# Two transformers' norms at the boundaries: x turned by a product with a diagonal of inverse norms

## The chip, the cores and the metric

One core of a Trainium2 chip runs one program. The metric is the device time of one execution in microseconds (us). [...] VectorE, ScalarE and GpSimd work on vectors, and SyncE's queue issues the loads.

## The reference

Two blocks of two layers each run one after the other on x (256 tokens of 1024 features, fp32). Each of the four layers is a mixer (stick-breaking attention, forgetting attention, differential attention with a context, short convolution) and a gated feed-forward part of 2816 features. In the first block the output of each part is normed before it is added:

```python
x = x + gt * rmsnorm(o, g_post)          # first block; the second: h = h + g * y
h = modulate(rmsnorm(x, g_pre), sh, sc)  # x / sqrt(mean(x*x) + eps) * g, then * (1 + sc) + sh
```

So between every two parts there is a boundary: the product's result o is gated and added to x, x is normed over its 1024 features, scaled and shifted by columns that come from c, and goes into the next product.

## The kernel before

x lies in SBUF as two tiles of 128 tokens (t = 0, 1) by 1024 features. The products take features on partitions, so at each boundary x must be turned. There are eight boundaries with work, b = 1 to 8; b = 8 only adds. Odd ones lead from a mixer to a feed-forward part, even ones to the next mixer. Weights stream as 1 MB chunks through four buffers (`raw`); ScalarE rounds each half chunk (`whi`, line 1213), VectorE takes the rest (`wlo`, line 1720), and TensorE makes three products for each pair of such parts. Six halves are kept.

Each engine's order is written out by hand, and engines wait for counters. At a boundary, for each tile t and half c of the features:

- ScalarE squares the product o (b <= 4 alone) and, once x is updated, x, with a sum over the half (line 1268, `scalar_square`). Behind the first half it makes sum / 1024 + eps (line 1271); behind the second the logarithm (1278) and exponential (1280), which leaves the inverse norm.
- VectorE multiplies o with the gate row (`vector_gated`, 1819 and 1816), adds it to x (`vector_added`, 1828 or 1831), and scales x by the inverse norm into `xn` (`vector_scale`, 1838, two halves).
- TensorE turns `xn` in 128x128 tiles into PSUM (`transposes`, 752), by pairs p = 0 to 3 of two tiles. Two pairs that both ScalarE and VectorE need at the same time are turned twice ("both"), into two banks.
- ScalarE or VectorE scales and shifts a pair (`scalar_pair` 1234, `vector_pair` 1793), ScalarE rounds it (`scalar_high` 1248), VectorE takes the rest (`vector_low` 1804), and the next product may start.

The boundaries b = 2 and 4 go by tile (`BY_TILE`): the next stage's products of tile 0 run before tile 1 is normed, and tile 1 is turned amid them: six transposes of tile 0, four more behind the first products, then eight of tile 1. The five others (b = 1, 3, 5, 6, 7) turn both tiles first: eight transposes for tile 0, twelve for tile 1, and the products of lines 647 or 656 follow. `early` halves of weights are split amid a boundary where there is time.

Of the kernel before, what the change touches and what calls it, by code (L numbers as in the profile page):

```python
# [7 lines left out]
EPS = 1e-6  # L8
# [218 lines left out]
def build(nc, A, out):  # L227
# [3 lines left out]
    with stack:  # L231
# [38 lines left out]
        ncum = sb("ncum", [H, S])  # L270
        mat = stack.enter_context(nc.psum_tensor("mat", [P, 8, 512], f32))
# [17 lines left out]
        s_sq, s_pow, s_pow0, s_row = (sem(n) for n in ("s_sq", "s_pow", "s_pow0", "s_row"))  # L289
# [120 lines left out]
        def pair_by(b, t, p):  # L410
            if b in BY_TILE:
                return "both" if (t, p) == (0, 0) else "act" if t == 0 or p < 2 else "dve"
            if t == 0:
                return "act" if p < 2 else "dve"
            return "both" if p < 2 else "act"

        def pair_bank(b, t, p, copy=0):
# [5 lines left out]
            if t == 0:  # L423
                return (4, 256 * p) if p < 2 else (7, 256 * (p - 2))
# [4 lines left out]
        SQ, POW, ROW, PROD = {}, {}, {}, {}  # L429
        TMA, TMD, HH, HL, TR = {}, {}, {}, {}, {}  # L430
        sums = 0
        for b in range(9):
# [12 lines left out]
            for key in squares:  # L445
                SQ[(b,) + key] = len(SQ) + 1
                if b:
                    sums += 1 if key[2] == 0 else 2
                    POW[(b,) + key] = sums
# [4 lines left out]
            elif by_tile:  # L454
                rows = ["b00", "b01", "c00", "c01", "xn00", "xn01", "b11", "c10", "c11", "xn10", "xn11"]
            elif low:
                rows = ["b00", "b01", "c00", "c01", "xn00", "xn01", "b10", "b11", "c10", "c11", "xn10", "xn11"]
            else:
                rows = ["b00", "c00", "b01", "c01", "b10", "c10", "xn00", "xn01", "b11", "c11", "xn10", "xn11"]
# [286 lines left out]
        def transposes(b, t, first, last, copy=0):  # L746

            for p in range(first, last + 1):
                pe.wait_ge(s_row, ROW[b, f"xn{t}{p // 2}"])
                o, at = pair_bank(b, t, p, copy)  # L750
                for j in range(2):
                    m = pe.transpose(bank(o)[:, at + P * j:at + P * j + P], xn[:, t, (2 * p + j) * P:(2 * p + j + 1) * P],
                                     ident[:, :])
# [503 lines left out]
        def scalar_square(b, kind, t, c):  # L1257
# [10 lines left out]
            act.activation(y, src, ACT.Square, accum_out=at).then_inc(s_sq, 1)  # L1268
            act.wait_ge(s_sq, SQ[b, kind, t, c])
            if c == 0:  # L1270
                act.activation(at, at, ACT.Identity, bias=epsc[:, :], scale=1.0 / D).then_inc(s_pow, 1)
                return

            ahead = epsc[:, :]
            if not whole:
                act.wait_ge(s_pow, POW[b, kind, t, 0])
# [3 lines left out]
            act.activation(at, at, ACT.Exp, scale=-0.5).then_inc(s_pow, 1)  # L1280

        def scalar_boundary(b, early=0):
# [17 lines left out]
            scalar_pair(b, 0, 1)  # L1300
# [533 lines left out]
        def vector_scale(b, t):  # L1834
            dve.wait_ge(s_pow, POW[b, "x", t, 1])
            for c in range(2):
# [620 lines left out]
```

## Time and profile before

| | |
|---|---|
| median of 3 runs | 1368.39 us (1364.52, 1368.39, 1372.63) |
| the profiled execution | 1364.44 us |
| its span, first to last instruction | 1363.1 us |
| busy: TensorE, VectorE, ScalarE, GpSimd | 95%, 79%, 56%, 3% |
| granted clock of TensorE over the span | 0.989 |

The profile is one execution. A row of a timeline gives the start and the duration in us, the engine (PE is TensorE, DVE VectorE, ACT ScalarE, POOL GpSimd), the line, the operation, what it writes and reads, how many alike follow each other, and in brackets how long the engine sat idle ahead of it and who ended that. A matmul's duration holds its way through the array, so matmuls that follow each other overlap; their distance is the difference of starts. The granted clock is 1.00 at 2.4 GHz and 0.50 at 1.2 GHz.

### The profile page before, as it was taken

What the parts mean: (1) busy time and instruction counts of PE and PEld (TensorE: products, weight loads), DVE (VectorE), ACT (ScalarE), POOL (GpSimd) and SP (SyncE); (2) the same over time, 40 slices, a digit from 0 to 9 for tenths busy, and PEclk for the clock granted to TensorE, in tenths of its full rate; (3) what the DMA queues carried; (4) which work ended last, traced back from release to release, by engine and by line L of the source; (5) the groups of instructions that cost most, each with busy time, mean ns of one, the idle gap of its engine ahead of it and who ended that gap; (6) DMA issues with size and microseconds to landing.
All of it is one profiled execution on the core that took longest, in us unless ns stands there. A gap on an engine that the chain in (4) does not pass through costs nothing.

```text
span 1363.1 us, 20647 instructions
## 1 busy us (share of the span) xinstructions
PE 1297.8 (95%) x8024; PEld 1134.4 (83%) x8024; DVE 1080.2 (79%) x1691; ACT 768.2 (56%) x1330; POOL 45.2 (3%) x74
## 2 busy tenths in 40 slices
PE   4999899999999889999989999899999899999998
PEld 3898799998798689998777776688878799788887
DVE  6887788887868788889887877788888887777753
ACT  4755845553856675554675667755543644655541
POOL 0022000000014100000000000000000000000000
PEclk9999999999999989999999999899999999899999
DMA  9966587679577544667835342177789576347560
GB/s 374 375 243 225 186 296 287 264 293 361 199 293 282 194 155 178 256 261 275 312 124 187 138 163 85 63 277 276 280 306 361 214 282 258 124 185 279 216 227 35
DMA packets 46738, 319.96 MB, mean 235 GB/s; under 512 B 5216, under 2 KB 5808, under 8 KB 9648
## 3 DMA queue, kind: packets, MB, share of 16 engines
q1 hardware_dynamic: 46640, 318.63, 61.9%
q8 instruction: 64, 1.05, 0.3%
q14 instruction: 34, 0.28, 0.1%
HBM read 317.51 MB, written 1.10 MB: 234 GB/s over the span
## 4 chain that ended last, share of the span: by engine, by line
PE 57%; DVE 21%; ACT 8%; DMA 8%; issue 5%; SPq 0%; POOL 0%; ACTq 0%; DVEq 0%; POOLq 0%
PE mat L659 9%; DVE wlo L1720 8%; PE mat L732 6%; PE mat L734 6%; PE mat L736 6%; PE mat L658 5%; ACT whi L1213 4%; DVE raw L1747 4%; PE mat L694 4%; PE mat L696 4%; PE mat L695 4%; DMA raw<-in_down 2%; DVE tmp L2267 2%; DMA raw<-in_mod 2%; PE mat L1102 2%
## 5 line engine op out<-in xcount | busy, mean ns | idle before, releaser
L1720 DVE TENSOR_TENSOR wlo<-raw,whi 128x1024 fp32r<-128x1024 f32 x393 | 474.5, 1223 | 141.9 <-ACT whi L1213 140.5
L1213 ACT ACTIVATE whi<-raw 128x1024 fp32r<-128x1024 f32 x393 | 403.9, 1051 | 183.0 <-DMA raw<-in_down 69.1
L694 PE MATMUL mat<-hHL,whi 128*128 128x256 f32 x1080 | 308.2, 285 | 3.5 <-DVE tmp L2267 3.4
L695 PE MATMUL mat<-hHL,whi 128*128 128x256 f32 x1080 | 305.5, 283 | 0.0
L696 PE MATMUL mat<-hHL,wlo 128*128 128x256 f32 x1080 | 305.5, 283 | 0.0
L1747 DVE SCALAR_TENSOR_TENSOR raw<-raw,cB 128x1024 f32<-128x1024 f32 x180 | 218.1, 1222 | 10.3 <-DMA raw<-in_mod 10.0
L659 PE MATMUL mat<-hHL,whi 128*128 128x512 f32 x616 | 222.8, 400 | 0.0
L694 PEld LDWEIGHTS mat<-hHL,whi 128*128 128x128 f32 x1080 | 207.1, 192 | 8.1 <-DVE tmp L2267 4.7
L695 PEld LDWEIGHTS mat<-hHL,whi 128*128 128x128 f32 x1080 | 207.2, 192 | 0.1
L696 PEld LDWEIGHTS mat<-hHL,wlo 128*128 128x128 f32 x1080 | 207.1, 192 | 0.0
L658 PE MATMUL mat<-hHL,wlo 128*128 128x256 f32 x616 | 173.6, 282 | 0.0
L659 PEld LDWEIGHTS mat<-hHL,whi 128*128 128x128 f32 x616 | 117.4, 191 | 24.3
L658 PEld LDWEIGHTS mat<-hHL,wlo 128*128 128x128 f32 x616 | 118.0, 192 | 4.2
L732 PE MATMUL mat<-whi,aHL 128*128 128x512 f32 x352 | 113.4, 392 | 4.0 <-DVE tmp L2275 2.3
L734 PE MATMUL mat<-wlo,aHL 128*128 128x512 f32 x352 | 112.4, 389 | 0.0
L736 PE MATMUL mat<-whi,aHL 128*128 128x512 f32 x352 | 112.4, 389 | 0.0
L732 PEld LDWEIGHTS mat<-whi,aHL 128*128 128x128 f32 x352 | 65.6, 188 | 20.7 <-DVE wlo L1720 4.7
L736 PEld LDWEIGHTS mat<-whi,aHL 128*128 128x128 f32 x352 | 66.1, 188 | 13.8
L734 PEld LDWEIGHTS mat<-wlo,aHL 128*128 128x128 f32 x352 | 66.1, 188 | 13.6
L2288 DVE TENSOR_TENSOR aHL<-tmp,aHL 128x512 fp32r<-128x512 f32 x44 | 30.5, 692 | 30.7 <-ACT aHL L1680 15.4
L1708 ACT ACTIVATE aHL<-tmp 128x512 fp32r<-128x512 f32 x22 | 13.9, 632 | 66.5 <-DVE tmp L2286 66.5
L732 PE MATMUL mat<-whi,oHL 128*128 128x512 f32 x128 | 45.5, 406 | 3.9 <-DVE oHL L2190 2.1
(237 smaller groups left out, 1882.0 us busy)
## 6 DMA issues: line engine op xcount, KB each, us to landing
raw<-in_mod SPq DMA_DIRECT2D x89, 1024.0 KB, 5.3
raw<-in_qkv SPq DMA_DIRECT2D x46, 1024.0 KB, 7.0
raw<-in_gate SPq DMA_DIRECT2D x44, 1024.0 KB, 5.3
raw<-in_up SPq DMA_DIRECT2D x44, 1024.0 KB, 5.1
raw<-in_down SPq DMA_DIRECT2D x44, 1024.0 KB, 6.1
raw<-in_wo SPq DMA_DIRECT2D x16, 1024.0 KB, 4.9
begin<-in_mod SPq DMA_DIRECT2D x6, 1024.0 KB, 17.1
gtb<-gates SPq DMA_DIRECT2D x8, 512.0 KB, 7.0
```

The source lines that it names most:

```text
L658: pe.matmul(o[:, 0:256], wl, hH[:, k, :], start=False, stop=False)
L659: return pe.matmul(two(o), wh, hHL[:, :, k, :], start=False, stop=(k == KT - 1))
L694: pe.matmul(o, wh[:, k, :], hH[:, k, :], start=(k == 0), stop=False)
L695: pe.matmul(o, wh[:, k, :], hL[:, k, :], start=False, stop=False)
L696: m = pe.matmul(o, wl[:, k, :], hH[:, k, :], start=False, stop=(k == KT - 1))
L732: pe.matmul(bank(2 * t + c), left, wh[:, 512 * c:512 * c + 512], start=(k == 0), stop=False)
L734: pe.matmul(bank(2 * t + c), left, wl[:, 512 * c:512 * c + 512], start=False, stop=False)
L736: m = pe.matmul(bank(2 * t + c), low, wh[:, 512 * c:512 * c + 512], start=False, stop=(k == nk - 1))
L1213: act.activation(whi[:, n % NSPL, :], raw[:, f % NRAW, 1024 * h:1024 * h + 1024], ACT.Copy).then_inc(s_hi, 1)
L1720: dve.tensor_tensor(out=wlo[:, n % NSPL, :], in0=raw[:, f % NRAW, 1024 * h:1024 * h + 1024], in1=whi[:, n % NSPL, :].bitcast(f32), op=ALU. ...
L1747: dve.scalar_tensor_tensor(out=src if last else prod[:, :], in0=src, scalar=1.0, in1=cB[:, c, :], op0=ALU.mult, op1=ALU.mult, accum_out=mo ...
L2288: dve.tensor_tensor(out=aL[:, 2 * j:2 * j + 2, :], in0=y, in1=aH[:, 2 * j:2 * j + 2, :].bitcast(f32), op=ALU.subtract).then_inc(s_al, 1)
```

## The change

At b = 1 to 7 VectorE no longer scales x. ScalarE multiplies the identity with the column of inverse norms (a 128x128 diagonal matrix, `diag`, one for each tile) and TensorE multiplies x itself by it, which turns and scales at once. What was a transpose is now a plain fp32 matmul with x as the stationary operand. GpSimd makes sum / 1024 + eps of the first halves, behind a counter of its own, `s_pre`. In the whole boundaries, the pair p = 1 of tile 0 moves from ScalarE to VectorE and into a bank of its own. The start (b = 0) keeps its transposes.

```diff
+        diag = sb("diag", [P, 2, P])
...
             if t == 0:
-                return "act" if p < 2 else "dve"
+                return "act" if p == 0 else "dve"
...
             if t == 0:
-                return (4, 256 * p) if p < 2 else (7, 256 * (p - 2))
+                return (4 + p, 0) if p < 2 else (7, 256 * (p - 2))
...
         def transposes(b, t, first, last, copy=0):
 
+            pe.wait_ge(s_diag, DIAG[b, t])
             for p in range(first, last + 1):
-                pe.wait_ge(s_row, ROW[b, f"xn{t}{p // 2}"])
                 o, at = pair_bank(b, t, p, copy)
                 for j in range(2):
-                    m = pe.transpose(bank(o)[:, at + P * j:at + P * j + P], xn[:, t, (2 * p + j) * P:(2 * p + j + 1) * P],
-                                     ident[:, :])
+                    m = pe.matmul(bank(o)[:, at + P * j:at + P * j + P], x[:, t, (2 * p + j) * P:(2 * p + j + 1) * P],
+                                  diag[:, t, :], start=True, stop=True)
             m.then_inc(s_tr, 1)
...
             act.activation(y, src, ACT.Square, accum_out=at).then_inc(s_sq, 1)
+            if c == 0:
+                return
             act.wait_ge(s_sq, SQ[b, kind, t, c])
-            if c == 0:
-                act.activation(at, at, ACT.Identity, bias=epsc[:, :], scale=1.0 / D).then_inc(s_pow, 1)
-                return
 
             ahead = epsc[:, :]
             if not whole:
-                act.wait_ge(s_pow, POW[b, kind, t, 0])
+                act.wait_ge(s_pre, PRE[b, kind, t])
                 ahead = (post_stat if kind == "o" else norm_sum)(b, t, 0)
             act.activation(at, at, ACT.Ln, bias=ahead, scale=1.0 / D).then_inc(s_pow, 1)
             act.wait_ge(s_pow, POW[b, kind, t, 1] - 1)
             act.activation(at, at, ACT.Exp, scale=-0.5).then_inc(s_pow, 1)
+            if kind == "x":
+                act.wait_ge(s_pow, POW[b, kind, t, 1])
+                act.activation(diag[:, t, :], ident[:, :], ACT.Copy, scale=at).then_inc(s_diag, 1)
...
             scalar_square(b, "x", 1, 1)
-            scalar_pair(b, 0, 1)
             scalar_high(b, 0, 0, 1, 2)
...
-        def vector_scale(b, t):
-            dve.wait_ge(s_pow, POW[b, "x", t, 1])
-            for c in range(2):
-                cs = slice(512 * c, 512 * c + 512)
-                dve.tensor_scalar(xn[:, t, cs], x[:, t, cs], norm_sum(b, t, 1), None, ALU.mult).then_inc(s_row, 1)
...
+            vector_pair(b, 0, 1)
             vector_pair(b, 0, 2)
             vector_pair(b, 0, 3)
-            vector_scale(b, 1)
...
+        def pool_first_half(b):
+
+            for kind, t in [key[1:] for key in PRE if key[0] == b]:
+                y = (post_stat if kind == "o" else norm_sum)(b, t, 0)
+                pool.wait_ge(s_sq, SQ[b, kind, t, 0])
+                pool.tensor_scalar(y, y, 1.0 / D, EPS, ALU.mult, ALU.add).then_inc(s_pre, 1)
...
+            for b in (1, 2):
+                pool_first_half(b)
             for h in range(H):
                 pool_forgetting(h)
+            for b in range(3, 8):
+                pool_first_half(b)
```

## Rows read from the trace of the kernel before

**Rows 1.** The page, part 1: busy time, share of the span, instructions.
```profile
PE 1297.8 (95%) x8024; PEld 1134.4 (83%) x8024; DVE 1080.2 (79%) x1691; ACT 768.2 (56%) x1330; POOL 45.2 (3%) x74
```

**Rows 2.** Waits: who waited for whom, total us, times, longest.
```profile
PE mat L752 <- DVE xn L1838: 16.8, 7, 4.1
```

**Rows 3.** Timeline of boundary 1, from ScalarE, VectorE and TensorE.
```profile
151.38 0.29 ACT L1271 ACTIVATE st<-st,epsc 128x1 f32<-128x1 f32 x1
...
156.77 0.61 ACT L1268 ACTIVATE xn<-x 128x512 f32<-128x512 f32 x1
...
157.83 0.20 ACT L1280 ACTIVATE st<-st 128x1 f32<-128x1 f32 x1
...
155.03 1.41 DVE L1828 SCALAR_TENSOR_TENSOR x<-xn,st,x 128x512 f32<-128x512 f32 x2
...
158.06 0.88 DVE L1838 TENSOR_SCALAR xn<-x,st 128x512 f32<-128x512 f32 x2 [0.35 <-ACT st L1280]
...
158.61 2.82 PE L752 MATMUL mat<-ident,xn 128*128 128x128 f32 x12 [4.09 <-DVE xn L1838]
161.16 0.55 PE L647 MATMUL mat<-hHL,whi 128*128 128x256 f32 x1
```

**Rows 4.** Windows: stretch, length, busy PE, PEld, DVE, ACT, POOL; granted clock, DMA share, GB/s.
```profile
158.60:162.00 3.40, 3.39 (x16) 3.29 (x17) 3.07 (x9) 3.28 (x11) 0.00 (x0) 0.50 0.00 0
...
350.00:367.00 17.00, 15.35 (x74) 12.01 (x74) 14.30 (x25) 16.14 (x40) 0.00 (x0) 1.00 0.35 132
...
482.80:489.60 6.80, 5.85 (x26) 5.51 (x27) 5.27 (x15) 6.56 (x20) 0.00 (x0) 0.50 0.06 20
...
672.00:690.00 18.00, 13.79 (x67) 10.70 (x66) 14.20 (x27) 15.93 (x42) 0.00 (x0) 1.00 0.37 145
...
878.80:885.60 6.80, 6.04 (x21) 4.94 (x20) 5.58 (x13) 6.74 (x15) 0.00 (x0) 0.50 0.00 0
...
1073.40:1076.70 3.30, 2.93 (x14) 2.83 (x15) 3.07 (x9) 3.18 (x11) 0.00 (x0) 0.50 0.01 2
...
1172.40:1179.10 6.70, 6.03 (x21) 4.92 (x20) 5.43 (x13) 6.64 (x15) 0.00 (x0) 0.50 0.01 1
```

**Rows 5.** Timeline of TensorE in the by-tile boundaries 2 and 4.
```profile
353.69 0.82 PE L752 MATMUL mat<-ident,xn 128*128 128x128 f32 x6
...
362.33 0.50 PE L732 MATMUL mat<-whi,hHL 128*128 128x512 f32 x1 [0.47 <-DVE wlo L1720]
...
688.63 0.50 PE L1102 MATMUL mat<-whi,hHL 128*128 128x512 f32 x1 [1.37 <-DVE hHL L1804]
```

**Rows 6.** Windows of TensorE alone: length, busy (matmuls), clock, DMA share, GB/s.
```profile
881.50:885.40 3.90, 3.90 (x13) 0.50 0.00 0
886.10:890.00 3.90, 3.90 (x24) 1.00 0.71 256
```

**Rows 7.** Timeline of TensorE at boundaries 3, 5 and 7.
```profile
486.55 0.55 PE L647 MATMUL mat<-hHL,whi 128*128 128x256 f32 x1
...
877.63 1.78 PE L752 MATMUL mat<-ident,xn 128*128 128x128 f32 x12 [2.46 <-DVE xn L1838]
...
880.17 0.77 PE L656 MATMUL mat<-hHL,whi 128*128 128x512 f32 x1 [0.76 <-DVE hHL L1804]
...
1173.80 0.76 PE L656 MATMUL mat<-hHL,whi 128*128 128x512 f32 x1 [0.68 <-DVE hHL L1804]
```

**Rows 8.** Groups of ScalarE by shape: busy us, mean ns, idle before.
```profile
L1234 ACT ACTIVATE tmp<-mat,modc 128x128 f32<-128x128 f32 x60 | 24.0, 451 | 3.2 <-PE mat L752 2.5
...
L1644 ACT ACTIVATE tmp<-cB 128x128 f32<-128x128 f32 x11 | 3.4, 310 | 0.3
```

**Rows 9.** Timeline of GpSimd in the start's norm.
```profile
13.59 0.62 POOL L2296 TENSOR_SCALAR st<-st 128x1 f32<-128x1 f32 x1 [0.21 <-ACT xn L1354]
```

**Rows 10.** Timeline of TensorE: eight transposes; seven records of fp32 products.
```profile
478.58 1.03 PE L752 MATMUL mat<-ident,xn 128*128 128x128 f32 x8
...
771.81 0.94 PE L1173 MATMUL mat<-att,xn 128*128 128x128 f32 x7
```

More of the change, by code:

```diff
@@ L286, in build @@
         s_hi, s_lo, s_tma, s_tmd, s_hh, s_hl = (sem(n) for n in ("s_hi", "s_lo", "s_tma", "s_tmd", "s_hh", "s_hl"))
-        s_sq, s_pow, s_pow0, s_row = (sem(n) for n in ("s_sq", "s_pow", "s_pow0", "s_row"))
+        s_sq, s_pow, s_pow0, s_row, s_diag, s_pre = (
+            sem(n) for n in ("s_sq", "s_pow", "s_pow0", "s_row", "s_diag", "s_pre"))
         s_step, s_mod, s_take, s_gate_out, s_gate_in = (sem(n) for n in (
@@ L423, in pair_bank @@
             if t == 0:
-                return (4, 256 * p) if p < 2 else (7, 256 * (p - 2))
+                return (4 + p, 0) if p < 2 else (7, 256 * (p - 2))
             return (2 * p + copy, 0) if p < 2 else (7, 256 * (p - 2))
         PAIRS = [(0, p) for p in range(4)] + [(1, p) for p in range(4)]
-        SQ, POW, ROW, PROD = {}, {}, {}, {}
+        SQ, PRE, POW, ROW, PROD, DIAG = {}, {}, {}, {}, {}, {}
         TMA, TMD, HH, HL, TR = {}, {}, {}, {}, {}
@@ L447, in build @@
                 if b:
-                    sums += 1 if key[2] == 0 else 2
-                    POW[(b,) + key] = sums
+                    if key[2] == 0:
+                        PRE[(b,) + key[:2]] = len(PRE) + 1
+                    else:
+                        sums += 2
+                        POW[(b,) + key] = sums
+                    if key[0] == "x" and key[2]:
+                        DIAG[b, key[1]] = len(DIAG) + 1
             if b == 0:
@@ L454, in build @@
             elif by_tile:
-                rows = ["b00", "b01", "c00", "c01", "xn00", "xn01", "b11", "c10", "c11", "xn10", "xn11"]
+                rows = ["b00", "b01", "c00", "c01", "b11", "c10", "c11"]
             elif low:
-                rows = ["b00", "b01", "c00", "c01", "xn00", "xn01", "b10", "b11", "c10", "c11", "xn10", "xn11"]
+                rows = ["b00", "b01", "c00", "c01", "b10", "b11", "c10", "c11"]
             else:
-                rows = ["b00", "c00", "b01", "c01", "b10", "c10", "xn00", "xn01", "b11", "c11", "xn10", "xn11"]
+                rows = ["b00", "c00", "b01", "c01", "b10", "c10", "b11", "c11"]
             for name in rows:
@@ L1847, in vector_boundary @@
                 lo(early)
-                vector_scale(b, 0)
                 vector_gated(b, 1, 0)
@@ L1858, in vector_boundary @@
                 vector_added(b, 1, 0)
-                vector_scale(b, 0)
                 vector_gated(b, 1, 1)
                 vector_added(b, 1, 1)
+            vector_pair(b, 0, 1)
             vector_pair(b, 0, 2)
             vector_pair(b, 0, 3)
-            vector_scale(b, 1)
             vector_low(b, 0, 0, 1)
@@ L1878, in vector_by_tile @@
             lo(1)
-            vector_scale(b, 0)
             vector_pair(b, 0, 0)
@@ L1889, in vector_by_tile @@
                 lo(1)
-                vector_scale(b, 1)
                 lo(1)
@@ L1894, in vector_by_tile @@
                 vector_low(b, 0, 3)
-                vector_scale(b, 1)
                 lo(1)
```

## The prediction, made before the changed kernel ran

> **What bounds the kernel now.** I read the page first: TensorE is busy 95% of the span, VectorE 79% and ScalarE 56% [rows 1]. So the time is TensorE's work plus its holes, and the question for a change at the boundaries is where the holes lie. The list of waits answers it: the seven waits of the transposes on VectorE's scaled rows, `xn` from line 1838, are the longest item, 16.8 us [rows 2]. I then read the boundaries one by one in order of time. Seven of the eight are changed (b = 1 to 7). Two of them, b = 2 and 4, go "by tile", and there TensorE has products to do meanwhile; the other five are "whole" and stop TensorE.
>
> Boundary 1 is the pattern for the whole ones [rows 3]. ScalarE takes the last of the two squares of tile 1 at 156.77, its logarithm at 157.50, its exponential at 157.83 (done 158.03); VectorE scales from 158.06; TensorE starts the twelve transposes of tile 1 at 158.61, after 4.09 us of nothing, and the next stage's products at 161.16. So a boundary's price is (a) when tile 1's transposes start, (b) how long they take, (c) at which clock the products behind them run.
>
> For (c) I read the granted clock in stretches [rows 4]. It is 0.50 (1.2 GHz) for some 3.4 us at b = 1 and 6 and some 6.8 us at b = 3, 5 and 7, every time behind a hole of 2.4 to 4.1 us between the two tiles' transposes, and 1.00 (2.4 GHz) throughout b = 2 and 4, whose holes are 1.4 us or less [rows 5]. In two equal stretches of the same product stage TensorE begins 13 matmuls at the half clock and 24 at the full one [rows 6]: a microsecond of products at half clock would be 1 - 13/24 = 0.46 us shorter at the full one. The half-clock product time behind the five boundaries is 0.8 (b = 1, 161.16 to 162.0), 3.1 (b = 3, 486.55 to 489.6), 5.4 (b = 5, 880.17 to 885.6), 0.4 (b = 6, 1076.33 to 1076.7) and 5.3 us (b = 7, 1173.80 to 1179.1) [rows 3, 4, 7]. That is 15.0 us, of which 6.9 are to be had: more than all other terms.
>
> **The change part by part.**
> 1. VectorE's scaling goes: 28 x 0.439 us, since a pair takes 0.88 [rows 3]. Most of these 12.3 us lie while others are waited for; on the path are only the second tile's. From the exponential's end to the first transpose are 158.61 - 158.03 = 0.58 us [rows 3].
> 2. ScalarE makes the diagonal: one copy of 128x128 with a scale, not in this trace. Below it lies a 128x1 operation, 0.20 (the exponential [rows 3]); above, a 128x128 from PSUM with scale and bias, 0.451; nearest is a 128x128 square from SBUF, 0.310 [rows 8]. I take 0.34, with 0.03 ahead and 0.09 to TensorE: 0.46 for 0.58, so -0.12 per tile, between -0.26 and +0.0.
> 3. The first halves' means go to GpSimd. On ScalarE each takes 0.29 [rows 3], of which the next instruction overlaps 0.1, and has a wait ahead: 0.2 to 0.33 us. GpSimd's slower operation of this kind took 0.62 [rows 9]; with 0.1 to get there it is done some 0.75 us behind the sum, and the logarithm that needs it comes 0.66 or more behind it, because the second half's square (0.62 and the reading of its sum) lies between. So it is hidden, at worst 0.1 us late. Nothing is queued behind these waits but the forgetting masks, and they stand between boundaries 2 and 3. What it gives depends on whether VectorE's rows are there: at b = 1 the second square comes at 156.4, when its rows are written (155.03 + 1.41), for 156.77 [rows 3]: -0.37; at b = 3 at 481.65 for 481.91, -0.26; at b = 5, 6 and 7 the square waited for VectorE anyway, 0.
> 4. Every transpose becomes an fp32 product of x with the diagonal. The price comes from the other fp32 products here: they leave two records each, 0.111 apart ((0.94 - 0.275) / 6), where a transpose leaves one and they come (1.03 - 0.27) / 7 = 0.109 apart [rows 10]. So 0.222 for 0.109. 136 transposes would cost 15.4 us more, but on the path are: tile 1 of the whole boundaries, and those of the by-tile ones. At half clock a record takes 0.213: 12 in 2.55 [rows 3].
> 5. The pair (0, 1), two operations of 0.451 [rows 8] less their overlap, moves from ScalarE, where it stood between tile 1's exponential and the high parts, to VectorE, beside tile 1's squares: 0. No DMA is issued or moved; SyncE's loads of gate rows wait for the same sums of VectorE as before, which come no later.
>
> Part 4 also acts on the hole. Tile 0's products last 8 x 0.222 = 1.8 us where the transposes took 0.9, in time that is idle. But ScalarE's pair (0, 0) waits for four of them together, 0.45 us later than now, and at b = 5, 6, 7 it stands ahead of tile 1's second square: +0.03, +0.14, +0.14.
>
> The Trainium skill (TensorE: Matmul & The Clock Gate, Terms) says that transpose mode is four times faster for fp32. The record of a transpose at 0.109 and the two records of an fp32 product at 0.222 say twice; by the page a product would be 0.44 and tile 1's twelve 5.3 us, which is the price of rival C. I take the rows.
>
> **The sum**, in starts of the next products, tile 1's 24 records at full clock being 2.67 us:
> - b = 1: tile 1 starts at 158.61 - 0.37 - 0.12 = 158.1. The hole is 154.9 to 158.1, 3.2 us, so I let the clock fall at 158.56 and rise at 162.0 as it did: 4 records at full, 16 at half, 4 at full clock end at 162.4. Now products start at 161.16, of which 0.8 us at half clock are worth 0.4: +0.85.
> - b = 3: start at 483.4, hole 2.7 us. I let the clock fall at 482.8 and, since there is now more behind it, rise 3.4 us later as at b = 1: products at 487.45, all at full clock, for 486.55 with 3.1 us at half: +0.9 - 1.4, about -0.6.
> - b = 5: start at 877.55; 24 records end at 880.2, products at 880.3 for 880.17. The hole shrinks from 2.46 [rows 7] to 1.8, near the 1.4 at which the clock stayed up. If it stays: 5.4 x 0.46 = 2.5, so -2.4.
> - b = 6: start as now, hole 1.5 with the gate row between, records end at 1076.45: +0.1 - 0.2 = -0.1.
> - b = 7: hole 1.8, products at 1174.0 for 1173.80, 5.3 x 0.46 = 2.4: -2.3.
> - b = 2: the norm of tile 0 is hidden behind the products; the six transposes at 353.69 become 0.67 longer and VectorE's half of pair 0 comes 0.45 later; VectorE's next steps move by 0.23 to the weights awaited at 362.33 [rows 5], and the eight products behind them cost 0.9 on TensorE with nothing waiting: +1.1.
> - b = 4: the products of pairs 2 and 3 of tile 0 put ScalarE's steps back by 0.9, of which its squares keep 0.8; the eight of tile 1 start 0.2 later, and pair (1, 0), which now waits 0.9 us for them and not 0.45, reaches the product at 689.75 for 688.63 [rows 5]: +1.1.
>
> Sum: 0.85 + 1.1 - 0.6 + 1.1 - 2.4 - 0.1 - 2.3 = -2.35 us. The products behind a boundary run at TensorE's own pace (busy 3.90 of 3.90 us [rows 6]), so I expect the sum to stay in the span. The profiled execution took 1364.44 with a span of 1363.1; it would be 1362.1. It lies 3.95 below the median of 1368.39, so I predict 1366.0. The three runs lie 8 us apart, and what this kernel's measurement can tell from no change is about 0.5%, 6.8 us.
>
> **The rivals.**
> - A, the clock stays up at all five: speaks for it that all holes shrink and that products, not transposes, fill the ends; against it the holes of 3.2 and 2.7 us at b = 1 and 3. Then b = 1 is -0.5 + 0.12 - 0.37 = -0.75 and b = 3 -0.37 - 0.13 - 1.4 = -1.9: sum -5.3, 1363.1. The clock did come back behind a stretch at b = 6 that was transposes but for its last 0.4 us [rows 4, 7]. The Trainium skill (same page, Part 4) says that transposes do not count as activity for the clock as products do; that stretch speaks against it, and if it held it would speak for this rival.
> - B, the clock falls at b = 5 and 7 all the same, for as long: the 4.9 us are not gained and part of the records there run at half clock, about 0.9 in all: +3.4, 1371.8. The hole of 1.8 us is above the 1.4 that is known to be harmless.
> - C, slower: tile 1's records run at half clock from first to last, and the clock stays down as long as now. 24 x 0.213 = 5.1 us where 2.55 are now, at five boundaries: +2.1, +2.0, +2.2, +2.6, +2.5, with +2.2 by tile +13.6, 1382. It decides from the third such boundary on. For it: the clock was at half through tile 1's transposes at b = 1, 3 and 6 [rows 4]. Against it: the holes shrink, and more work under a half clock should bring it back sooner, as at b = 1 and 6.
> - D, the second record of a product hides under the first: tile 1's records 1.3 us shorter, of which the chain through the pairs lets 0.3 pass, by tile nothing lost, and the clock up: about -9, 1359.5. Against it: fp32 products stand 0.222 apart everywhere here.
>
> **How the numbers follow.** Forecast 0.50, A 0.15, B 0.15, C 0.12, D 0.08. Forecast, A and B make 0.80: from 1359 to 1374, each with the spread of the runs. Faster by over 0.5% (below 1361.5): D and the lower tails, 0.18. Slower (above 1375.2): C and a little, 0.13. Within: 0.69.
>
> **What would show it.** Twice the records on the transposes' line, 0.111 apart; tile 1's first record 0.46 us behind the exponential's end; no half clock near b = 5, 6 and 7, products behind b = 5 at 24 in 3.9 us from the start; b = 2 and 4 longer by 1.1 us each. I am wrong if the clock's falls do not follow the holes, if GpSimd's mean is late, or if tile 0's longer products hold up more than pair (0, 0).

## The result, and the profile of the changed kernel

The changed kernel takes 1371.18 us, median of 16 runs (1366.78 to 1374.49). The kernel before took 1366.78, median of the 16 runs beside them (1362.29 to 1372.63). The ratio is 1.0032, 95% interval [1.0021, 1.0042]: 0.3% slower, where I forecast 0.2% faster (1371.18 lies inside my range of 1359 to 1374, with the wrong sign). Two more sets of runs of the same kernel, on two other chips, gave 1.0059 [1.0038, 1.0081] and 1.0039 [1.0024, 1.0053]. The loss is small, but it is there.

The profiled execution of the changed kernel is the fastest of its 16: 1366.78, span 1365.5. That of before was 2.3 us under its own median too. One profile of each can't carry a difference of 4 us, so several profiles of each kernel are laid side by side below.

The page, part 1, and the granted clock over 40 slices of the span, which was 1.00 nearly throughout; they answer to [rows 1]:

```profile
PE 1304.7 (96%) x8160; PEld 1142.6 (84%) x8160; DVE 1071.6 (78%) x1673; ACT 762.4 (56%) x1314; POOL 54.2 (4%) x94
...
PEclk9999999999999999999999999999999999999999
```

TensorE has 136 records more, VectorE 18 operations fewer, GpSimd 20 more. The wait of 16.8 us for scaled rows [rows 2] is now one of 11.4 us for the diagonal (view: waits):

```profile
PE mat L759 <- ACT diag L1289: 11.4, 7, 3.0
```

Boundary 1, timeline of ScalarE, then GpSimd, then TensorE, against [rows 3]:

```profile
152.37 0.29 ACT L1284 ACTIVATE st<-st 128x1 f32<-128x1 f32 x1 [0.52 <-POOL st L2302]
...
156.66 0.63 ACT L1275 ACTIVATE xn<-x 128x512 f32<-128x512 f32 x1
...
157.74 0.20 ACT L1286 ACTIVATE st<-st 128x1 f32<-128x1 f32 x1
157.97 0.40 ACT L1289 ACTIVATE diag<-ident,st 128x128 f32<-128x128 f32 x1
...
151.27 1.01 POOL L2302 TENSOR_SCALAR st<-st 128x1 f32<-128x1 f32 x1 [4.03 <-ACT xn L1275]
153.99 0.19 POOL L2302 TENSOR_SCALAR st<-st 128x1 f32<-128x1 f32 x1 [1.71 <-ACT xn L1275]
156.80 0.19 POOL L2302 TENSOR_SCALAR st<-st 128x1 f32<-128x1 f32 x1 [2.61 <-ACT xn L1275]
...
153.39 2.05 PE L759 MATMUL mat<-diag,x 128*128 128x128 f32 x16 [0.35 <-ACT diag L1289]
158.43 2.94 PE L759 MATMUL mat<-diag,x 128*128 128x128 f32 x24 [2.99 <-ACT diag L1289]
161.13 0.36 PE L654 MATMUL mat<-hHL,whi 128*128 128x256 f32 x1
```

Tile 1's first record starts 0.49 us behind the exponential's end (157.74 + 0.20), where it was 0.58. The diagonal's copy takes 0.40. The 24 records of tile 1 stand (2.94 - 0.27) / 23 = 0.116 apart. The hole between the tiles is 2.99 and not 4.09 us, and the clock did not fall. The next stage begins at 161.13 for 161.16. Windows of the stretches that were at half clock [rows 4], moved to where the boundary now lies; columns as there:

```profile
158.60:162.00 3.40, 3.40 (x30) 3.28 (x30) 2.93 (x9) 3.09 (x10) 0.00 (x0) 1.00 0.00 0
...
482.80:489.60 6.80, 4.53 (x37) 4.33 (x38) 6.26 (x18) 6.36 (x20) 0.19 (x1) 1.00 0.29 116
...
876.70:883.50 6.80, 5.08 (x42) 4.85 (x43) 5.57 (x15) 5.75 (x19) 0.32 (x1) 1.00 0.00 1
...
1073.40:1076.70 3.30, 2.91 (x22) 2.46 (x20) 2.15 (x5) 1.93 (x6) 0.19 (x1) 1.00 0.01 2
1172.40:1179.10 6.70, 5.09 (x44) 4.77 (x42) 6.07 (x16) 5.47 (x17) 0.00 (x0) 1.00 0.00 1
```

So all five whole boundaries kept the full clock in this execution: rival A's picture, with rival C's sign. Boundaries 5 and 7, then the by-tile ones 2 and 4 (TensorE; against [rows 5, 7]):

```profile
876.82 2.05 PE L759 MATMUL mat<-diag,x 128*128 128x128 f32 x16 [0.62 <-ACT diag L1289]
880.48 2.94 PE L759 MATMUL mat<-diag,x 128*128 128x128 f32 x24 [1.61 <-ACT diag L1289]
883.18 0.48 PE L663 MATMUL mat<-hHL,whi 128*128 128x512 f32 x1
...
1175.69 2.94 PE L759 MATMUL mat<-diag,x 128*128 128x128 f32 x24 [1.61 <-ACT diag L1289]
1178.39 0.48 PE L663 MATMUL mat<-hHL,whi 128*128 128x512 f32 x1
...
354.50 1.50 PE L759 MATMUL mat<-diag,x 128*128 128x128 f32 x12
...
358.42 1.05 PE L759 MATMUL mat<-diag,x 128*128 128x128 f32 x8
...
691.64 0.50 PE L1109 MATMUL mat<-whi,hHL 128*128 128x512 f32 x1 [1.15 <-DVE hHL L1812]
```

To see where the time went I counted the same records in every trace (transposes, products with the diagonal and idle products left out) and took the length of each stretch between two fixed records: seven stretches bN around the boundaries (a whole one with the 60 records behind it, where a half clock costs), and the stretches ahead of them. The table gives each length less that of before's first profile, in us; "up" says that the clock stayed up there, a number in brackets for how many us it was at half (both for b1, b3, b5 and b7 alone).

```
stretch  before   changed kernel (3 profiles)    before again   before, idle products
..b1     135.9    +0.09    +0.54    +0.94        +0.82          +0.19
b1        18.6    -0.30up  -0.30up  +2.19(6.8)   +0.91(6.8)     -0.01up
..b2     177.4    +0.96    -0.34    +0.84        -0.97          +0.62
b2        25.9    +0.84    +0.83    +0.84        -0.04          -0.04
..b3     100.0    -0.01    +1.22    +1.19        +1.12          +0.02
b3        23.2    -1.54up  +1.09(6.8) -0.19(3.4) -0.97(3.4)     -0.96up
..b4     175.0    +1.96    +5.32    +2.11        +3.85          +6.32
b4        26.0    +0.95    +0.92    +0.92        -0.01          +0.04
..b5     172.0    -0.21    -0.18    -0.20        +0.09          -0.08
b5        25.0    -1.98up  -1.99up  -2.01up      -0.85(6.8)     -2.01up
..b6     170.2    +3.22    +3.27    +3.45        -0.10          +0.38
b6        20.6    +0.39    +0.38    +0.39        -0.01          -0.03
..b7      76.2     0.00     0.00     0.00         0.00           0.00
b7        26.6    -2.03up  -2.01up  -2.01up      -1.99(3.4)     -2.06up
..end    172.3     0.00     0.00     0.00         0.00           0.00
```

The columns are the first profile and those of e1_after_again and e5_after_third; e12_before_third; e4_before_filled (below). Before's first profile itself had 3.4 us at half clock at b1 and 6.8 at each of b3, b5 and b7 [rows 4]. Three things stand out. b2, b4 and b6 are longer by the same amount in every profile of the change. The stretch ahead of b4 was shorter in before's first profile than in any of the changed kernel's, or in a second profile of before: it was a lucky one. And the stretch ahead of b6 is 3.2 to 3.5 us longer in all three profiles of the change and in neither of the others.

### The profile page after: what moved, and what is told of

Same layout as the page of the kernel before. It is cut to its first block, busy times and chain, and to the rows that moved or that the text cites. A ratio compares the mean times of both kernels' runs of the same rounds, so it can differ in the third digit from the quotient of the medians.

```text
span 1365.5 us, 20905 instructions
## 1 busy us (share of the span) xinstructions
PE 1304.7 (96%) x8160; PEld 1142.6 (84%) x8160; DVE 1071.6 (78%) x1673; ACT 762.4 (56%) x1314; POOL 54.2 (4%) x94
## 4 chain that ended last, share of the span: by engine, by line
PE 60%; DVE 19%; ACT 9%; DMA 7%; issue 4%; POOL 0%; SPq 0%; ACTq 0%; DVEq 0%; POOLq 0%
DVE wlo L1728 8%; PE mat L701 7%; PE mat L703 7%; PE mat L702 7%; PE mat L739 5%; PE mat L666 5%; PE mat L741 5%; PE mat L743 5%; ACT whi L1220 5%; DVE raw L1755 4%; DMA raw<-in_down 4%; PE mat L665 3%; PE mat L1109 2%; PE mat L1111 2%; PE mat L1110 2%
## 5 line engine op out<-in xcount | busy, mean ns | idle before, releaser
L666 PE MATMUL mat<-hHL,whi 128*128 128x512 f32 x616 | 219.6, 396 | 0.0
```

What stands on the lines that cost most here:

```text
L666: return pe.matmul(two(o), wh, hHL[:, :, k, :], start=False, stop=(k == KT - 1))
```

## The experiments

18 runs followed; each has the kernel before beside it on its own chip (1365.4 to 1367.0 us), and ratios are to that. The changed kernel itself stood beside e2 to e4 (e1) and beside e6 and e7 (e5) alone; the other variants of it are compared with it by their ratios.

**Repeats.** No edit, the changed kernel twice and the kernel before twice.

> The changed kernel as it is, for a second profile beside the first, whose granted clock of 0.999 and time of 1366.8 us are the best of its 16 runs. Theory 1 (the clock falls in holes at whole boundaries in most executions and then catches twice as many records): clock 0.990 to 0.995, a fall at boundaries 1 or 3, tile 1's records at 0.213 us there, 1368 to 1374 us, ratio 1.003. Theory 2 (the second records cost alike in every execution, the clock is no part of it): boundaries as in the first profile, whatever the clock. Theory 3 (the time is lost between boundaries, where weights arrive late): the boundaries as in the first profile, and another hole of 1 us or more at the end of a feed-forward part.

1372.38 us, 1.0059 [1.0038, 1.0081]. Of the boundaries the third alone has a fall (theory 1), and the stretch ahead of b4 is 5.3 us longer (theory 3).

> The changed kernel once more, as the measure for the two partial ones on this chip and as a third profile. So far two profiles: boundaries together 3.7 and 1.1 us shorter than in the profile before, the stretches between them 6.0 and 9.8 us longer. Theory 1 (what a boundary gives is lost again where weights arrive late, in the same places every time): boundaries 1 to 5 us shorter, between 5 us or more longer, among it 2 to 3 us at the turn from up to down in layer 2. Theory 2 (the stretches between differ by chance and the second records are the whole cost): between near 0 to 4 us, and then the total below 1368 us.

1371.83 us, 1.0039 [1.0024, 1.0053]. The seven boundaries together are 0.1 us longer than in before's first profile, not 1 to 5 shorter; the stretches between them are 8.3 us longer. So neither theory gives both parts. At boundary 1 the clock fell as tile 1's records began, and they ran at half clock (TensorE, against the 2.94 us of the first profile):

```profile
159.14 5.49 PE L759 MATMUL mat<-diag,x 128*128 128x128 f32 x24 [2.99 <-ACT diag L1289]
```

> The kernel before against itself: a ratio of 1.000 within 0.001, and a second profile. If the stretches between boundaries differ from the first profile by 2 to 6 us, as those of all four other profiles do, then the first profile was a lucky one between boundaries and the changed kernel's 6 to 10 us there are mostly no effect of the change.

1367.31 us, 0.9995 [0.9981, 1.0010]. No profile of it is used.

> The kernel before, unchanged, for another profile of it. If its first profile was an ordinary one, the stretches between the boundaries agree with it within 1 us each but for the clock's falls; if it was a lucky one (it is 2.4 us under its median), the stretches ahead of boundaries 4 and 6 are 1 to 5 us longer here, and part of what the changed kernel's profiles show there is not the change's.

1365.39 us, 0.9999 [0.9989, 1.0009]: two kernels that are the same come out the same, so 0.3% is told apart here. Its profile settles boundary 7 (timeline of TensorE, then windows of TensorE alone):

```profile
1171.56 1.04 PE L752 MATMUL mat<-ident,xn 128*128 128x128 f32 x8
1175.14 2.75 PE L752 MATMUL mat<-ident,xn 128*128 128x128 f32 x12 [2.54 <-DVE xn L1838]
1177.68 0.77 PE L656 MATMUL mat<-hHL,whi 128*128 128x512 f32 x1
```

```profile
1168.00:1175.30 7.30, 4.76 (x26) 1.00 0.00 1
1175.30:1178.70 3.40, 3.40 (x16) 0.50 0.00 0
1178.70:1185.00 6.30, 6.30 (x38) 1.00 0.04 7
```

The transposes and the hole of 2.54 us are those of [rows 7]'s execution, but the half clock lasts 3.4 us and not 6.8, and ends 1.0 us behind the first product. The boundary is as short as the changed kernel's (-1.99 for -2.03) with nothing changed. The gain that I forecast there belonged to the other profile.

**Parts taken out of the change, or done alone.**

e2, the second records left out: transposes of the unscaled x in the same place (so the norm's scaling is missing, and nothing else).
```
- m = pe.matmul(bank(o)[...], x[...], diag[:, t, :], start=True, stop=True)
+ m = pe.transpose(bank(o)[...], x[...], ident[:, :])
```


> The changed kernel with transposes of unscaled x by the identity in place of the products with the diagonal (so the norm of x is left out of what follows; every wait is the same, the diagonal is made and waited for). It takes away the second records alone. Theory 2: each by-tile boundary shorter by 0.9 to 1.1 us and each whole one by 1.3: in all 7 to 9 us under the changed kernel, some 1363 us, ratio to before 0.996. Theory 1: the clock falls behind the holes of 2.4 us or more as in the kernel before, so the whole boundaries gain only their earlier start: 0.998 to 1.000. Theory 3: within 0.2% of the changed kernel, 1.002.

1364.78 us, 0.9992 [0.9979, 1.0004], and 7.6 us under the changed kernel on the same chip. Without the doubled records the whole loss is gone. Theory 2 has the size (7 to 9 us), but not its parts: the whole boundaries are not 1.3 us shorter each (b1 is +0.39 here, b3 -1.32, b7 -2.13). b4 and b6 fall to +0.25 and +0.09 and the stretch ahead of b6 to +0.60, but b2 stays at +0.83. So the records are not what makes b2 longer, or not alone. The changed kernel's first profile shows what else is late there (timeline of GpSimd, VectorE and ScalarE):

```profile
361.76 1.35 POOL L2302 TENSOR_SCALAR st<-st 128x1 f32<-128x1 f32 x1 [8.51 <-ACT xn L1275]
...
361.83 1.22 DVE L1728 TENSOR_TENSOR wlo<-raw,whi 128x1024 fp32r<-128x1024 f32 x1
...
363.20 0.29 ACT L1284 ACTIVATE st<-st 128x1 f32<-128x1 f32 x1 [0.86 <-POOL st L2302]
```

GpSimd's mean of tile 1 ends at 363.11, 0.06 behind the end of VectorE's subtraction of the weights (363.05), and ScalarE, with its next weight split and the diagonal behind it, has waited 0.86 us. At boundary 1 the mean of 1.01 us, 151.27 to 152.28, likewise ends 0.05 behind such a subtraction (151.01 and 1.22 us long); the three means of 0.19 us there (147.05, 153.99, 156.80) have no such subtraction beside them.

e3, the kernel before with GpSimd making the first halves' means; e17, the changed kernel with them back on ScalarE.
```
+ pool.tensor_scalar(y, y, 1.0 / D, EPS, ALU.mult, ALU.add)            (e3)
+ act.activation(at, at, ACT.Identity, bias=epsc[:, :], scale=1.0 / D)  (e17)
```


> The kernel before with the first halves' means on GpSimd and nothing else changed: the part that I put at -0.37 us at boundary 1, -0.26 at 3 and 0 at 5, 6 and 7. Expected from all theories: 0.999 to 1.000. If GpSimd's mean comes late behind the sum, some 0.1 us at each of 20 first halves or more, 1.001 or above.

1366.57 us, 1.0012 [1.0002, 1.0021]: above the 1.000 at most that every theory had, so the branch of the late mean came.

> The changed kernel with the first halves' means back on ScalarE (Identity with 1/D and the bias), each waiting for its own sum. Theory (the second records are the cost): within 2 us of the changed kernel, ratio to the kernel before 1.002 to 1.006. Rival (GpSimd's means carry a good part of the loss): 1.5 us or more under it, ratio 1.000 to 1.002.

1373.85 us, 1.0063 [1.0042, 1.0083] over 6 runs. The means as a whole are no part of the loss that these runs can tell: alone they add 0.1%, taken away they give nothing back. b2 is +0.91 without them, and +0.83 with them and without the second records. But the late mean by itself is not enough: with VectorE's scaling at boundary 2 and the mean as late (0.86 us) in e3, b2 is +0.20 (+0.21 in e6, +0.18 in e11). What e2 has beyond these is the diagonal on ScalarE. From the start of tile 1's first square to ScalarE's next weight split are 2.13 us in before, 2.68 in e3 and 3.11 in e2: 0.55 for the mean, 0.43 for the diagonal. So the second records, or the mean and the diagonal together, are each enough to make b2 late, and they don't add up. The stretch ahead of b6 is +3.48 again.

e6, e7, e11, e13, e14: VectorE's scaling and the transposes back at some boundaries (GpSimd's means stay; the pair (0, 1) goes back to ScalarE in e7 alone).
```
+ def OLD(b): return b in (2, 4)      # e6; e7: b not in (2, 4); e11: b not in (5, 7); e13: b == 4; e14: b == 5
+ if OLD(b): vector_scale(b, t), then pe.transpose(..., xn[...], ident[:, :])
```


> The changed kernel with boundaries 2 and 4 as before (VectorE's scaled rows, transposes; GpSimd's means stay). I put the new way at +1.1 us at each. Its two profiles give +0.84 and +0.95 at them. If the boundaries' terms add up in the time: 1.8 to 2.2 us under the changed kernel on this chip. If what is saved at a boundary is lost between them: under 1 us.

1367.35 us, 0.9999 [0.9987, 1.0011]. 4.5 us under the changed kernel, more than either branch had.

> The changed kernel with boundaries 1, 3, 5, 6 and 7 as before (scaled rows, transposes, pair (0, 1) on ScalarE; GpSimd's means stay): the complement of e6. Theory 1 (second records in the whole boundaries slow the kernel, the clock they keep up gives nothing back): 4 to 6 us under the changed kernel, 1.002 of the kernel before. My forecast's way of counting (these five boundaries give 4.5 us): 4 us over the changed kernel.

1368.61 us, 1.0008 [0.9996, 1.0020]. 3.2 us under the changed kernel: theory 1's direction at somewhat less than its 4 to 6, and the opposite of my forecast's way of counting.

The full change gave 1.0039 on this chip. Putting b = 2 and 4 back gives 4.5 us, though the two are only 0.84 + 0.92 = 1.76 longer; putting the other five back gives 3.2. The two halves of the change add up to 0.0 to 0.1% and together they cost 0.4%, so something depends on both. The stretch ahead of b6 is where it shows: +0.97 and 0.00 here, +3.45 with both. e7 shows one thing more. At boundary 7, which is the old way there, the hole is again 2.54 us, and the clock did not fall at all (timeline, then a window of all engines):

```profile
1179.15 1.53 PE L763 MATMUL mat<-ident,xn 128*128 128x128 f32 x12 [2.54 <-DVE xn L1861]
...
1170.00:1190.00 20.00, 16.31 (x92) 13.58 (x91) 16.26 (x31) 15.33 (x35) 0.31 (x2) 1.00 0.14 50
```

So the same transposes with the same hole had 6.8, 3.4 and 0 us at half clock in three executions.

> The changed kernel with the diagonal product at boundaries 5 and 7 alone, where each profile of the change shows the boundary 2 us shorter; boundaries 1, 2, 3, 4 and 6 have VectorE's scaling and the transposes back; GpSimd's means and pair (0,1) on VectorE stay. Theory 1 (a gain ahead of a stage that waits for weights is given back, but boundary 7 has none late behind it, its following stretch is equal in all kernels to 0.1 us): 1365 to 1367 against 1367 of the kernel before, ratio 0.998 to 1.000. Rival (each gain shows in full): 1363, ratio 0.997.

1365.45 us, 0.9994 [0.9982, 1.0005]. b5 and b7 are 1.98 and 2.01 shorter than in before's first profile, and the time is the same, as theory 1 has it. But b7 was as short in before's second profile, so most of these 4 us is no gain over an ordinary execution in the first place.

> The changed kernel with boundary 4 alone the old way. Theory (the wait for down weights behind boundary 5 needs the later boundary 4 together with the new boundary 5): boundary 4 gives back 0.9 us and the stretch ahead of boundary 6 falls from +3.3 to about +1 us, together 3 us: 0.2 to 0.3% under the changed kernel, 1367 to 1369 where the kernel before is at 1366. Rival (only the second records' own time counts): 0.9 us under the changed kernel, 1370.

1369.22 us, 1.0025 [1.0011, 1.0039]. The stretch ahead of b6 is +1.35, b4 is -0.01: in the profile as the theory has it. The time does not decide: the ratio lies inside the 1.0021 to 1.0042 of the changed kernel's first set, so the 3 us under it are not shown.

> The changed kernel with boundary 5 alone the old way. Theory: the stretch ahead of boundary 6 falls from +3.3 to 0 to +1 us, and boundary 5 gives back 0 to 1.1 us of its gain: 1 to 3 us under the changed kernel, 1367 to 1369. Rival (boundary 5 is a plain gain of 1 to 2 us and the stretch behind it does not hang on it): 1 to 2 us above the changed kernel, 1371 to 1372.

1370.58 us, 1.0041 [1.0023, 1.0059]. The stretch ahead of b6 fell to +0.68, as the theory has it, but the time did not fall with it: here the theory is half right at best. The profiled execution is the slowest of its seven (1374.86); it spends the difference at b1 (+2.21, clock low) and in the stretches ahead of b2 and b3 (+2.33 each), with the clock down seven times before its last 0.1 us.

**Clock and loads.**

e4 and e18: products of the identity with itself, written to an unused bank of PSUM (where TensorE's results go), between the tiles' records of the whole boundaries.
```
+ for i in range(14 if b <= 3 else 8):    # e4, kernel before;  e18, changed kernel: 8 if b <= 3 else 4
+     pe.matmul(bank(6)[:, 256:384], ident[:, :], ident[:, :], start=True, stop=True)
```


> The kernel before with idle fp32 products of the identity by itself (nobody reads them, a free part of PSUM) between tile 0's and tile 1's transposes of the whole boundaries: 14 at boundaries 1 and 3 (3.1 us in holes of 4.1), 8 at 5, 6 and 7 (1.8 us in holes of 2.5). If the clock follows those holes: no fall at boundaries, granted clock 0.999, up to 6.9 us less, 1361 us, ratio 0.995 to 0.997. If the clock falls for another reason, or what it gives is lost again between boundaries: 0.999 to 1.000.

1365.85 us, 1.0008 [0.9995, 1.0022]. The mean clock over its 12 runs is 0.9962, for 0.9889 of the kernel before on that chip. That is 2 x 0.0073 x 1365 = 20 us less at half clock, and the time is the same: the second branch.

> The changed kernel with idle products of the identity between tile 0's and tile 1's records of the whole boundaries (8 at boundaries 1 and 3, 4 at 5, 6 and 7), so that the clock should stay up there; nothing is left out. Rival A of the prediction (half-clock time is worth 0.46 us for each us to the end): 2 to 4 us under the changed kernel, level with the kernel before. Theory (the stretches between the boundaries take it up, as in the filled kernel before): within 1.5 us of the changed kernel, ratio to the kernel before 1.002 to 1.006, with the mean clock at 0.997 or more.

1369.11 us, 1.0025 [1.0016, 1.0034], clock 0.9948 for the 0.9934, 0.9922 and 0.9927 of the changed kernel's three sets. It is not level with before; whether it is under the changed kernel is open, since the ratio lies inside the first set's 1.0021 to 1.0042 and under the other two. The clock did not reach the 0.997 of the theory, so this is a weak test of rival A: in the profiled execution it stayed up at all five whole boundaries, but fell at four other places. The stretch ahead of b6 is +0.86 here.

e9 and e10: the modulation loads beside the down and up weights of layers 1 and 2 cut to an eighth, in the kernel before and in the changed one (those modulations are sums over other data).
```
+ cols = 256 if item[0] == "mod" and item[1:3] in LIGHT else src.shape[-1]
- sp.dma_start(raw[:, i, 0:src.shape[-1]], src)
+ sp.dma_start(raw[:, i, 0:cols], src[:, 0:cols])
```


> The kernel before, with the modulation loads that fly beside the down and up weights of layers 1 and 2 cut from 1 MB to 128 KB each (20 loads: products 0 and 2 of layer 2, products 0, 2 and 3 of layer 3). Left out: seven eighths of those weights, so that these modulations are sums over other data; every instruction stays. Theory 1 (between the boundaries the kernel waits for weights that come late, and time won at a boundary is given back there): the stretches ahead of boundaries 4 and 6 shrink by 2 to 6 us each and the time falls by 4 to 12 us, to 1355 to 1363. Rival (the stretches are bound by TensorE, and the boundaries' gain went to something else): within 1.5 us of the kernel before.

1359.32 us, 0.9957 [0.9942, 0.9971], as theory 1 has it; the stretches ahead of b4 and b6 are -1.35 and -3.93.

> The same cut of 20 modulation loads in the changed kernel; the same part is left out. Theory 1: without the late weights the boundaries' own sum shows, so this one stands level with or up to 3 us under the cut kernel before, where the uncut ones stood 4.4 us apart the other way; its stretch ahead of boundary 6 no longer stands 3.2 us over. Rival (the second records cost in the stages whatever the loads do): it stays 3 to 6 us above the cut kernel before, as the uncut one does.

1365.12 us, 0.9988 [0.9978, 0.9998]. The kernel before does wait for weights: 6.8 us of it go with the bytes, 3.9 of them ahead of b6. But the rival holds for the pair: the changed kernel stays 5.8 us above. Ahead of b6 it stands 1.07 over now (-2.86 for -3.93), as much as its b5 is shorter (-1.98 for -0.91), and 4.4 ahead of b4, where ScalarE waits for an up chunk (timeline of e10):

```profile
580.71 1.06 ACT L1224 ACTIVATE whi<-raw 128x1024 fp32r<-128x1024 f32 x1 [3.99 <-DMA raw<-in_up]
```

e15 and e16: nothing left out, but those modulation products started earlier, beside gate and up.
```
- _spread([(2, 1)], halves(START["ffn", 1] + 8, START["ffn", 1] + 46))
- _spread([(2, 0), (2, 2)], halves(START["ffn", 1] + 46, START["ffn", 1] + 64))
+ _spread([(2, 1), (2, 0)], halves(START["ffn", 1] + 8, START["ffn", 1] + 46))
+ _spread([(2, 2)], halves(START["ffn", 1] + 46, START["ffn", 1] + 64))
...
+ _spread([(2, 5), (3, 1), (3, 0), (3, 2)], halves(START["ffn", 2] + 4, START["ffn", 2] + 44))
+ _spread([(3, 3)], halves(START["ffn", 2] + 44, START["ffn", 2] + 62))
```


> The kernel before with the modulation products of the down stages started earlier: product 0 of layer 2 beside gate and up of layer 1, products 0 and 2 of layer 3 beside gate and up of layer 2; only 8 products are left beside each down stage in place of 16 and 24 steps. Nothing is left out. If the down stages wait for loads and gate and up have room, some of the 6.8 us that the cut loads gave comes without cutting any: 1360 to 1364. Rival (gate and up have no room, the loads move the wait): 1365 to 1370.

1381.55 us, 1.0114 [1.0093, 1.0135]. A clear miss: gate and up have no room, and the stretches ahead of b4 and b6 grow by 10.2 and 7.9 us.

> The same earlier modulation products in the changed kernel. Theory: with the down stage of layer 2 less crowded the wait ahead of boundary 6 shrinks, and this stands 1 to 3 us above the spread kernel before (the records' own 1.75 us at boundaries 2 and 4 and 0.4 at 6, less up to 1.1 at 5). Rival: 4 us or more above it, as with the loads as they were; then the wait is not one of the crowded stage.

1383.99 us, 1.0152 [1.0128, 1.0177]. It stands 2.4 us above e15, as the theory has it, and the stretch ahead of b6 is the same in both (+7.91 and +7.89); but its five runs lie 9 us apart and don't exclude the rival. No complete version here beats the kernel before by more than the measurement tells.

**The wait ahead of b6.** Most of it, 2.5 of 3.3 us beside e12, is one hole, at the turn from up to down of layer 2; the rest arises some 50 us later, at another down chunk. Timeline of TensorE and ScalarE in the changed kernel, and windows of the hole and of the 3.4 us behind it:

```profile
1012.87 0.82 PE L739 MATMUL mat<-whi,aHL 128*128 128x512 f32 x2 [4.62 <-DVE tmp L2272]
...
1000.83 1.06 ACT L1220 ACTIVATE whi<-raw 128x1024 fp32r<-128x1024 f32 x1 [4.04 <-DMA raw<-in_down]
...
1010.00:1013.30 3.30, 0.43 (x2) 0.42 (x3) 3.27 (x6) 0.54 (x1) 0.00 (x0) 1.00 0.80 313
1013.30:1016.70 3.40, 3.40 (x10) 2.62 (x9) 3.40 (x5) 1.63 (x3) 0.00 (x0) 0.50 0.95 361
```

The same place in the kernel before: ScalarE in before's first profile, TensorE in e12 (whose clock also fell behind the hole, for 3.4 us):

```profile
997.71 1.06 ACT L1213 ACTIVATE whi<-raw 128x1024 fp32r<-128x1024 f32 x1 [2.74 <-DMA raw<-in_down]
...
1013.53 0.71 PE L732 MATMUL mat<-whi,aHL 128*128 128x512 f32 x2 [2.12 <-DVE tmp L2275]
```

In the changed kernel ScalarE waits 4.04 us for the first down chunk, where it was 2.74; what stands behind it on ScalarE comes late, and TensorE's hole is 4.62 for 2.12 us. The transfer itself is slower. These are the us from issue to landing of its megabyte, read from the DMA issues of each trace:

```
changed kernel: first profile 8.31, e1 8.38, e5 8.24, e17 8.15
without the full change, loads whole:
                before 7.01, e12 6.97, e2 7.15, e3 7.02, e4 6.95, e6 7.15, e7 7.02, e11 6.95, e13 6.90,
                e14 6.82, e18 6.97
```

That is a good half of it. The other part is when the load is issued. Counted from the end of stretch b5 it is issued at 98.5 us in the full change, for 97.5 in before's first profile and 97.3 in e12; 1.0 us later and 1.3 us slower make the 2.3 us by which TensorE's hole ends later than in before's first profile. The later issue comes with the new boundary 5 (98.5 to 98.7 in e6, e11, e13 and e18 too) and in part with an old one that was as short (97.8 to 98.1 in e3, e4 and e7, whose b5 is -1.7 to -2.0). In e10 beside e9, where the neighbouring loads are cut, the issue is again 1.0 us later (98.5 for 97.5), the transfer is equal (5.00 and 4.98), and what is left of the difference ahead of b6 is 1.07. So time won at boundary 5 is given back in part or in whole at this load, which starts earlier by less than the boundary ends.

Why the transfer takes some 1.2 us more in the full change and in none of the others, I could not show. Two other loads are in flight with it, the DMA engines move 346 to 361 GB/s over it in both kernels, and the issues stand at the same distances from each other within some tenths of a us. By single profiles it takes the later b4 and the new b5 together (e13, e14), and idle products in the holes of the whole boundaries undo it (e18).

## Why the prediction was wrong

- **Part 1, VectorE's scaling off the path**: right. 0.49 us from exponential to TensorE for 0.58.
- **Part 2, the diagonal's copy**: 0.34 taken, 0.40 measured at b = 1 and 402 ns as the mean of 14; inside the bounds. Each tile gains 0.09 and not 0.12.
- **Part 3, GpSimd hidden, at worst 0.1 us late**: wrong at b = 2, where it is 0.86 us late, and at tile 0 of b = 1, 0.52. Over the 20 means ScalarE waited 2.1 us, in 4 places. The mean takes 0.19 us by itself, less than the 0.62 I took, and up to 1.35 beside VectorE's subtraction of two SBUF tensors (SBUF is the on-chip memory that holds x and the weights). The Trainium skill (GPSIMD Engine Reference, Specifications) says that GpSimd's SBUF interface is shared with VectorE and contended by its instructions with two SBUF inputs; these rows agree, and by it the mean should have been priced at what is left of a subtraction, 1.22 us, wherever one can lie beside it. The price in the end was small, as e17 shows.
- **Part 4, second records**: right in kind and size: 8160 - 8024 = 136 records, 0.116 apart for 0.111. b = 2 and 4 grew by 0.84 and 0.93 where I had 1.1 each, but only b = 4 for the reason given (+0.25 without second records); at b = 2 the late mean and the diagonal together do as much without them. b = 6 grew by 0.39 where I had -0.1, and was +0.09 without second records; but it is also +0.39 in e7, with boundary 6 the old way, and +0.15 in e13 with the new, so what makes it longer is not shown.
- **Part 5, the pair (0, 1)**: no cost is seen; it was not tested by itself.
- **The clock**: the holes shrank (2.99, 2.75, 1.61 and 1.61 us at b = 1, 3, 5, 7) and there was no fall at b5 and b7 in any profile of the changed kernel. A hole of 1.6 us let the clock be in all of them; one of 2.5 us brings a fall in some executions and none in others (e7). Over all timed executions the mean clock rose from 0.989 to 0.992 to 0.993. At b = 1 and 3 it fell in some executions of the changed kernel and not in others, with the same holes of 2.99 and 2.75 us. The Trainium skill (TensorE: Matmul & The Clock Gate, Part 4) has transposes not count as activity; no run here shows it, and boundary 7 of e12, where the clock came back 3.4 us after its fall with transposes filling some 2.4 of them (1175.3 to 1178.7 at half, transposes from 1175.14 on), does not speak for it; nor does boundary 7 of e7, where it stayed up through them.
- **The sum**: this is where it failed, in two steps of it. The first is the terms -2.4 and -2.3 at b = 5 and 7. The arithmetic was right against before's first profile (-1.98 to -2.03), but the length of a fall, and whether it comes, is a matter of the single execution, and I took it from one. Beside the second profile of before the change gains 1.1 us at b5 and 0.0 at b7. Where the clock stays up in both kernels (the first profile of the change beside e4) the seven boundaries differ by -0.29, +0.88, -0.58, +0.91, +0.03, +0.42 and +0.03, which is +1.4 us: the change's own work is a small loss.
- The second is the sentence "I expect the sum to stay in the span", which rested on the stretch right behind a boundary and looked at none further on. A higher clock at the boundaries gave nothing in e4 (1.0008 with 20 us less at half clock), so the 6.9 us that I called "to be had" were not. And the stretch ahead of b6, in which I put nothing, lost 2.8 us beside e4's. 1.4 + 2.8 = 4.2 us, near the loss of 4.4 that was measured. It is an account from two single profiles, whose stretches ahead of b4 differ by 4.4 us the other way, and not a proof.
- **The rivals**: A's clock came at five boundaries in one profile, without its time: the seven boundaries together are 3.7 us shorter there, where A had 5.3, and the whole is not. B's falls at b5 and b7 didn't come, though its 1371.8 is by luck the nearest number. C's picture came at single boundaries of the whole ones, not at five: at b1 of e5 tile 1's records took 5.49 us and b1 is +2.19, where C had +2.1, and at b3 of e1 they took 5.49 too. D didn't come: no second record hides. The loss is of a kind that none of them had: records that cost 1.4 us at their own places and, as far as the profiles show, make a load far behind them later and slower.

What stays open: why the one transfer takes longer, whether e13 and e18 are faster than the changed kernel at all, why e14 got no time back, and why cutting the loads widened the distance between the kernels from 4.4 to 5.8 us (their intervals overlap there). That the second records as a whole are the cause is shown by e2; how much of their price each place takes is only read from profiles that differ by 1 to 4 us in the stretch ahead of b4 for reasons of their own.

## What to carry to other kernels

Take two or three profiles of the kernel before, before a term is built on something that comes and goes; a fall of the clock behind a hole is such a thing, and its length in one trace is not a gain to count on. In a kernel whose weights arrive just in time, time won at a boundary is not time won at the end: ask of each stretch behind it what it waits for, and put a record that doubles on the list of costs even where it fills a hole. If two halves of a change are harmless alone and cost together, look for the one wait that is longer only with both.

## What the runs showed of the hardware that I had not expected

- A GpSimd operation of 128x1 took 0.19 us by itself. Beside a VectorE subtraction of 1.22 us with two SBUF inputs it ended 0.05 to 0.06 us behind it, after 0.5 to 1.35 us (six means of the changed kernel's first profile); beside additions of two SBUF inputs (0.69 us, boundaries 5 and 6) it took 0.3 to 0.7.
- The clock's falls lasted 3.4 or 6.8 us, and the same transposes with the same hole (2.54 us at b = 7) showed either length in two executions of one kernel, and no fall in one of another (e7).
- A 1 MB load took 4.7 to 5.0 us from issue to landing when it flew nearly alone (the down chunk issued some 15 us later in the same traces) and 6.8 to 8.4 us (the first down chunk of layer 2) with two others in flight.
- 52 idle products in five holes raised the mean granted clock from 0.9889 to 0.9962 and changed the time by 0.08% [-0.05, +0.22].
